# A decoder block on one core: first adaLN columns in three parts, four weight units side by side at both norms, per-token sums for the first norm

## The reference, cut to what matters

```python
mod = silu(c) @ w_ada + b_ada                    # 6144 columns: shift1, scale1, gate1, shift2, scale2, gate2
h   = rms_norm(x, norm1_g) * (1 + scale1) + shift1
proj = h @ w_in                                  # 128 columns of it are a "unit": units 0 to 3 are q_lat (2), k_idx, w_idx
...                                              # sparse attention, gated linear recurrence, merge
x   = x + gate1 * (merged @ w_out)
h2  = rms_norm(x, norm2_g) * (1 + scale2) + shift2
x   = x + gate2 * (square(relu(h2 @ w_mlp1 + b_mlp1)) @ w_mlp2 + b_mlp2)
```

## Time and profile before

| | us |
|---|---|
| three executions | 963.65, 968.84, 968.44 |
| median | 968.44 |
| the profiled execution | 967.11 |
| its span (first to last instruction) | 965.4 |
| PE, DVE, ACT, POOL busy in it | 878.1, 464.7, 335.9, 233.0 |
| mean granted clock of TensorE | 0.950 of full speed |

### The profile page before, as it was taken

One profiled execution on the slowest core, in us unless ns is written; L12 is line 12 of the kernel. 1 busy time (PEld: TensorE's weight loads), 2 busy tenths in 40 slices (PEclk: granted clock), 3 DMA queues, 4 the chain that ended last, 5 costly groups with the idle time before them and its releaser, 6 DMA issues.

```text
span 965.4 us, 10903 instructions
## 1 busy us (share of the span) xinstructions
PE 878.1 (91%) x3855; PEld 688.1 (71%) x3855; DVE 464.7 (48%) x763; ACT 335.9 (35%) x495; POOL 233.0 (24%) x125
## 2 busy tenths in 40 slices
PE   3799899899877977988899996999999999999998
PEld 2577578687766764655568874688888888888886
DVE  4914789791887784444429764643211122221000
ACT  2634452453123313665512223434312124442211
POOL 3024233334000000000000000264444444444440
PEclk9699999999989977989889998999999999999999
DMA  9912323423111112222226653263233233333302
GB/s 358 254 54 72 82 66 87 107 54 101 25 38 27 44 27 82 66 83 71 66 66 202 199 187 108 68 195 108 89 93 103 87 97 99 89 107 97 99 22 87
DMA packets 144551, 95.69 MB, mean 99 GB/s; under 512 B 8199, under 2 KB 138629, under 8 KB 143493
## 3 DMA queue, kind: packets, MB, share of 16 engines
q1 hardware_dynamic: 143104, 95.18, 33.2%
q10 hardware_dynamic: 1412, 0.07, 0.1%
HBM read 93.13 MB, written 2.10 MB: 99 GB/s over the span
## 4 chain that ended last, share of the span: by engine, by line
PE 75%; DVE 18%; DMA 2%; ACT 2%; issue 2%; SPq 0%; DVEq 0%; ACTq 0%
PE bank L1100 19%; PE bank L1101 19%; PE bank L1102 19%; PE bank L1241 3%; PE bank L1242 3%; PE bank L1243 2%; DMA ada_raw<-in_w_ada 2%; PE bank L1318 2%; PE bank L1344 2%; DVE w_lo L753 2%; DVE hg_at L909 2%; DVE hg_rt L877 1%; DVE rt_k L805 1%; PE bank L1128 1%; DVE ada_acc L972 1%
## 5 line engine op out<-in xcount | busy, mean ns | idle before, releaser
L407 POOL TENSOR_TENSOR w_lo<-w_raw,w_hi 128x1024 fp32r<-128x1024 f32 x90 | 224.1, 2489 | 703.7 <-ACT w_hi L461 703.7
L1100 PE MATMUL bank<-h_hi,w_hi 128*128 128x512 f32 x544 | 219.3, 403 | 14.0 <-DVE h_lo L783 13.5
L1101 PE MATMUL bank<-h_lo,w_hi 128*128 128x512 f32 x544 | 213.6, 393 | 0.0
L1102 PE MATMUL bank<-h_hi,w_lo 128*128 128x512 f32 x544 | 213.3, 392 | 0.0
L461 ACT ACTIVATE w_hi<-w_raw 128x1024 fp32r<-128x1024 f32 x126 | 132.7, 1053 | 166.1 <-PE bank L1102 163.5
L1100 PEld LDWEIGHTS bank<-h_hi,w_hi 128*128 128x128 f32 x544 | 102.9, 189 | 45.7 <-issue 16.9
L1101 PEld LDWEIGHTS bank<-h_lo,w_hi 128*128 128x128 f32 x544 | 103.3, 190 | 21.9 <-issue 1.7
L1102 PEld LDWEIGHTS bank<-h_hi,w_lo 128*128 128x128 f32 x544 | 103.2, 190 | 21.7
L1100 PE MATMUL bank<-u_hi,w_hi 128*128 128x512 f32 x256 | 100.0, 391 | 0.0
L1102 PE MATMUL bank<-u_hi,w_lo 128*128 128x512 f32 x256 | 99.7, 389 | 0.0
L1101 PE MATMUL bank<-u_lo,w_hi 128*128 128x512 f32 x256 | 99.6, 389 | 0.0
(11 more groups left out here) (212 smaller groups left out, 1087.1 us busy)
## 6 DMA issues: line engine op xcount, KB each, us to landing
w_raw<-in_w_mlp SPq DMA_DIRECT2D x128, 256.0 KB, 3.0
w_raw<-in_w_in SPq DMA_DIRECT2D x88, 256.0 KB, 3.3
ada_even<-in_w_ada SPq DMA_DIRECT2D x20, 512.0 KB, 4.7
ada_raw<-in_w_ada SPq DMA_DIRECT2D x8, 1024.0 KB, 9.1
ada_odd<-in_w_ada SPq DMA_DIRECT2D x8, 512.0 KB, 4.5
w_raw<-in_w_out SPq DMA_DIRECT2D x16, 256.0 KB, 3.0
x_nat<-in_x SPq DMA_DIRECT2D x4, 512.0 KB, 6.3
w_raw<-in_w_proj_a SPq DMA_DIRECT2D x8, 256.0 KB, 2.8
```

The costliest lines, as they stand in the source:

```text
L407: nc.gpsimd.tensor_tensor(w_lo[:, s], w_raw[:, s], w_hi[:, s].bitcast(F32), ALU.subtract).then_inc(lo_ready, 1)
L1100: mm(bank[b][:], w_hi[:, slot, j], rhs_hi(i), start=f, stop=False)
L1101: mm(bank[b][:], w_hi[:, slot, j], rhs_lo(i), start=False, stop=False)
L1102: end = mm(bank[b][:], w_lo[:, slot, j], rhs_hi(i), start=False, stop=l)
```

## The change

At the first norm the shift1 and scale1 columns are loaded, summed, turned and used in three parts of the feature tiles: tiles 0 to 3, 4 and 5, 6 and 7. SP's order becomes x, part 0 (eight DMAs of 512 KB, rows of 2 KB), weight units 0 to 3, part 1 and part 2 (eight DMAs of 256 KB each, rows of 1 KB). The sum of squares is taken from x as it lies in natural order: ACT squares and sums each 128 tokens in one instruction (four of 128x1024), a root and a reciprocal over 128x4 follow, DVE puts the four columns on diagonals, and four matmuls with ones spread them over a bank, which `scaled` then reads. The squares of the transposed tiles and their sums on PE go. Units 0 to 3 lie in banks 0 to 3 and are worked tile by tile: `block(n, k, b)` is three matmuls. Unit 5 waits for fewer read-outs. The two Exps on the lower bound move on ACT from the first stage to the place after the q roots.

At the second norm the first four units of w_mlp1 lie in banks 0, 1, 4 and 5; all four take tiles 0 to 2 as they come, then each its tiles 3 to 7. `mod_columns(2)` moves from before the last unit of w_out to around the last sum of squares, and DVE's use of it to after the reciprocal.

```diff
+    PARTS = [(0, 4), (4, 6), (6, 8)]
-            for k in range(KC):
-                if k >= 4:
-                    sp.wait_ge(ada_used, k - 3)
-                sp.dma_start(ada_raw[:, k % 4], w_ada_v[0, k]).then_inc(ada_loaded[k % 4], 16)
+            def load_ada1(part):
+                c0, c1 = PARTS[part]
+                for k in range(KC):
+                    if part:
+                        sp.wait_ge(ada_used, 4 * (part - 1) + k // 2 + 1)
+                    sp.dma_start(ada_raw[part][:, k], w_ada_v[k, :, 0:2, c0 * P:c1 * P]
+                                 ).then_inc(ada_loaded[KC * part + k], 16)
+            load_ada1(0)
...
             load(3, 3, columns(w_in_v, 3, ds(C_WIDX, P)))
+            load_ada1(1)
+            load_ada1(2)
...
+            for b in range(TB):
+                act.wait_ge(x_loaded[b], 16)
+                nc.scalar.activation(x_sq[:, b], x_nat[:, b], ACT.Square, accum_out=XSS[:, b:b + 1]
+                                     ).then_inc(xss_ready, 1)
+            nc.scalar.activation(XRS, XSS, ACT.Sqrt, scale=1.0 / D, bias=EPSC).then_inc(rt_ready, 1)
...
+            split_hi(0)
+            split_hi(1)
+            for part, (k0, k1) in enumerate(PARTS):
+                act.wait_ge(mod_ready, part + 1)
+                for k in range(k0, k1):
+                    act.wait_ge(t_ready, k + 1)
+                    nc.scalar.activation(h_hi[:, k], tmp[:, k % 2], ACT.Identity,
+                                         bias=SHIFT1[:, k:k + 1]).then_inc(t_hi, 1)
+                    if k in (1, 2):
+                        split_hi(k + 1)
...
             for k in range(KC):
+                ada_sum(0, k)
+                if k == 4:
+                    dve.wait_ge(rt_ready, 1)
+                    dve.wait_ge(consts_ready, 1)
+                    step(v.reciprocal(XRS, XRS))
+                    for b in range(TB):
+                        end = v.tensor_scalar(xr_diag[:, b], ident[:], XRS[:, b:b + 1], None, ALU.mult)
+                    end.then_inc(diag_ready, 1)
...
+            split_lo(0)
+            split_lo(1)
...
+            mod_part(0)
+            dve.wait_ge(xT_ready, KC)
+            dve.wait_ge(xrs_spread, 1)
+            norm_split(xT, A1, bank[6][:], SHIFT1, h_hi, h_lo, 4)
+            split_lo(2)
+            split_lo(3)
+            for k in range(KC):
+                ada_sum(1, k)
+            for k in range(3):
+                ada_sum(2, k)
+            mod_part(1)
+            norm_split(xT, A1, bank[6][:], SHIFT1, h_hi, h_lo, 6, 4)
+            for k in range(3, KC):
+                ada_sum(2, k)
+            mod_part(2)
+            norm_split(xT, A1, bank[6][:], SHIFT1, h_hi, h_lo, KC, 6)
...
-                if g >= 2:
-                    pe.wait_ge(lin_evac, g - 1)
+                pe.wait_ge(lin_evac, g - 1 if g >= 6 else g - 3)
...
+            def block(n, k, b):
+                mm(bank[b][:], w_hi[:, n % WS, k], h_hi[:, k], start=k == 0, stop=False)
+                mm(bank[b][:], w_hi[:, n % WS, k], h_lo[:, k], start=False, stop=False)
+                end = mm(bank[b][:], w_lo[:, n % WS, k], h_hi[:, k], start=False, stop=k == KC - 1)
+                if k == KC - 1:
+                    end.then_inc(group_done, 1)
+            mod_part(0)
+            for ns_ in ((0, 1), (2, 3)):
+                pe.wait_ge(lo_ready, ns_[1] + 1)
+                for k in range(4):
+                    pe.wait_ge(t_lo, k + 1)
+                    for n in ns_:
+                        block(n, k, n)
+            mod_part(1)
+            for k in range(4, 6):
+                pe.wait_ge(t_lo, k + 1)
+                for n in range(WS):
+                    block(n, k, n)
+            mod_part(2)
+            for n in range(WS):
+                for k in range(6, KC):
+                    pe.wait_ge(t_lo, k + 1)
+                    block(n, k, n)
+            unit(4)
...
-                if m == KC - 2:
-                    mod_columns(2)
+            mod_columns(2, 0, 4)
             sum_square(11, False, True, ones, sq_o)
+            mod_columns(2, 4, 8)
+            for k in range(3):
+                pe.wait_ge(t_lo, T_U - KC + k + 1)
+                for n in range(4):
+                    block(U_1[0] + n, k, UP_BANK[n])
+            for n in range(4):
+                for k in range(3, KC):
+                    if n == 0:
+                        pe.wait_ge(t_lo, T_U - KC + k + 1)
+                    block(U_1[0] + n, k, UP_BANK[n])
```

More of the change, by code:

```diff
@@ L492, in root @@
                                      bias=EPSC).then_inc(rt_ready, 1)
[L494 to L505, removed]
+            act.wait_ge(vec_turned, 1)
+            nc.scalar.activation(col[:], bank[0][:, 0:P], ACT.Copy).then_inc(col_ready, 1)
+            split_hi(0)
[8 more added lines that the diff above has]
+                        split_hi(k + 1)
             take(0, latT[:, 0]); split_hi(4)
@@ L669, in _ @@
                 split_hi(U_O + m + WS)
-            root(11, 26, rt_o[:], D)
+            root(11, 18, rt_o[:], D)
             for k in range(KC):
@@ L754, in split_lo, with mod_part, pair @@
                                 ALU.subtract).then_inc(lo_ready, 1)
[L756 to L763 removed]
+            split_lo(0)
+            split_lo(1)
+            def mod_part(part):
+                k0, k1 = PARTS[part]
+                def pair(t):
+                    return t.rearrange("p (s k) -> p s k", s=2)[:, :, k0:k1]
+                dve.wait_ge(mod_turned, part + 1)
+                step(v.tensor_tensor(pair(mod[:, 0:2 * KC]), pair(bank[7][:, 0:2 * KC]),
+                                     pair(col[:, V_BADA:V_BADA + 2 * KC]), ALU.add))
+                v.scalar_tensor_tensor(out=A1[:, k0:k1], in0=SCALE1[:, k0:k1], scalar=1.0,
+                                       in1=col[:, V_G1 + k0:V_G1 + k1], op0=ALU.add,
+                                       op1=ALU.mult).then_inc(mod_ready, 1)
+                dve.wait_ge(mod_ready, part + 1)
             nt = [0]
@@ L1142, in _ @@
                 end.then_inc(x_turned, 1)
-                if k:
-                    sum_square(0, k == 1, False, ones)
-            sum_square(0, False, True, ones)
-            pe.wait_ge(ada_used, KC)
-            for j in range(2 * KC):
-                end = mm(bank[1][:, j:j + 1], ada_acc[:, j * P:(j + 1) * P], ones[:, 0:1], start=True,
-                         stop=True)
-            end.then_inc(mod_turned, 1)
-            pe.wait_ge(mod_ready, 1)
-            unit(0, before=lambda k: pe.wait_ge(t_lo, k + 1))
@@ L1153, in _, with mod_part @@
-            for n in (1, 2, 3, 4):
-                unit(n)
+                if k == 3:
+                    pe.wait_ge(diag_ready, 1)
+                    for b in range(TB):
+                        end = mm(bank[6][:, b * P:(b + 1) * P], ones[:], xr_diag[:, b], start=True, stop=True)
+                    end.then_inc(xrs_spread, 1)
+            pe.wait_ge(vec_loaded, 16 * 15)
+            nc.tensor.transpose(bank[0][:, 0:P], vec[:], ident[:]).then_inc(vec_turned, 1)
+            def mod_part(part):
+                pe.wait_ge(ada_used, KC * (part + 1))
+                for j in range(*PARTS[part]):
+                    for g in range(2):
+                        end = mm(bank[7][:, g * KC + j:g * KC + j + 1], ada_acc[:, g, j * P:(j + 1) * P],
+                                 ones[:, 0:1], start=True, stop=True)
+                end.then_inc(mod_turned, 1)
```

159 lines of the change are left out of this document (80 added, 79 removed).

## The result

| | before | changed |
|---|---|---|
| executions beside each other | 963.65, 968.84, 968.44, 968.05, 963.35 | 962.09, 962.21, 962.05, 958.60, 958.03 |
| median | 968.05 | 962.05 |
| the profiled execution, its span | 967.11, 965.4 | 962.09, 960.3 |
| mean granted clock in it | 0.950 | 0.948 |

The ratio is 0.9924, with a 95% interval of 0.9904 to 0.9944: faster by about 7.4 us by the ratio and by 6.0 by the medians. 959.3 was forecast, with a range of 954 to 966. The direction and the range held; of the 9.1 us in the sum two thirds to four fifths came.

A forecast was written before the change was run, and what follows sets the result against it. PE, with 75% of the chain, was taken as the bound, time being gained where it waits or runs slowly. 4.1 + 1.1 + 3.9 = 9.1 off 967.11 gives 958.0, as a median 959.3, range 954 to 966.

The forecast's parts named there:

- Start of the norm: First norm: DVE begins it at 27.1 instead of 40.76, with 13.7 gained at the start, 10 of it from bytes.
- lies behind DVE's sums: First stage: the root's spread by four matmuls on PE was taken as covered by DVE's column sums.
- Small sums: First norm, DVE: column sums of 512 elements for parts 1 and 2 at 0.68 each, bounds 0.60 and 0.80.
- Rival (b): First norm: DVE's small sums have a floor, at worst 1.2 each; gain only 0.8, 967.6; chance 0.09.
- Clock: First norm: PE's gaps before tiles 4 and 6 bring the low clock back, costing 4.2 (3.3 to 5.0) of 8.3.
- Rival (a): First norm: both gaps leave the clock high; gain 13.3, so 955.1; chance 0.12.
- Rival (d): First norm: bursts of 24 matmuls never bring the full clock back; 5.2 slower, 973.6; chance 0.05.
- The mark: First norm: unit 3 read out at about 70.1 in the kernel before, the point its gain was measured from.
- Unit 5: After the first norm: unit 5 no longer waits for a read-out behind a square on ACT, gaining 1.1.
- rival (c): First stage DMA: short rows flow at the weights' 296 GB/s, norm 3.5 to 4 late; gain 5.3, 963.1; chance 0.11.
- Second norm: Tile 0 reaches PE 1.3 earlier and four units share the tiles: unit 3 read out at 625.8 against 629.7, gaining 3.9.
- Between the norms everything hangs on PE's flow and moves along: Stages between the two norms: assumed to shift along with PE, with no gain or loss entered for them.

The follow-up runs named there:

- after_again: The changed kernel run once more, unchanged: 960.89, ratio 0.9926 to the kernel before.
- first_norm_only: The changed kernel with its second norm put back as before: 965.83, ratio 0.9977 to the kernel before.
- fill_tuned: Changed kernel plus unused matmuls (fillers) at both norms, sums of squares of k and q, and attention heads 0, 3, 5, 7: 943.33, ratio 0.9725.
- two_parts_tuned: fill_tuned with the first norm's columns in two parts of four tiles, 10 fillers ahead of the turn, 12 behind: 944.04, ratio 0.9760.

## Why the prediction was right, and where it was off

**Start of the norm** (27.1, was 29.09). The bytes were right: part 0 was out of the way as a bound. The step that was short is "ACT's last copies and `col` end near 23.2": from the diagonals it allowed 4.4 and the trace has 6.3 (19.16 to 25.45). PE's spread of the root takes 2.08 of it, which "lies behind DVE's sums" had as covered, and the sixteen transposes of tiles 4 to 7 take 3.43 (21.23 to 24.66), so the last copy begins at 24.68 and everything behind follows it. They take 0.21 each; in the kernel before four start within 0.44, 0.11 each:

```profile
25.42 0.60 PE L1140 MATMUL bank<-ident,x_nat 128*128 128x128 f32 x4
25.86 1.02 PE L1128 MATMUL bank<-sq,ones 128*128 128x512 f32 x2
```

Half the pace looks like the low clock, but the row of the granted clock does not show it: in the changed kernel it reads 1.00 there. The cause of the slow transposes stays open.

```profile
21.30:24.60 3.30, 3.30 (x17) 1.00 1.26 267
```

Besides, a sum of 1024 elements has a pitch of 1.38 (14.04 - 12.66), not 1.2: I had taken overlap off where a dependent instruction adds 0.09 of waiting. These sums ended before the copies, so this did not set the start.

**Small sums** (0.68, was 0.85). Eleven of them took 37.5 to 46.0, 8.5 for 7.4. The instruction is 0.76, inside my bounds of 0.60 to 0.80; the pitch lies outside, because the bounds were durations and the list moves at the pitch of a chain. Rival (b) at 1.2 did not come.

**Clock.** In this profile it fell in both gaps, as forecast, and the runs with fillers price the two at about 2.9 (1.4 to 3.9 between single profiles) for 4.2 taken, with bounds of 3.3 to 5.0. The low stretches ran from 49.0 to 52.4 and from 59.3 to 62.6. Rival (a) is answered with the same runs: with a clock that stays up, about 3 more would have come. Half of it did come in `after_again`, where the gap ahead of tile 4 left the clock high. Rival (d) did not come: the clock was back within 4 us of each restart here, within 6 in `first_norm_only`. Against the sheet, tile 4 reached PE 1.9 late and tile 6 3.6 late; since the restarts cost less, the last group ends at 66.65 instead of 66.0. That this is so near is two errors of opposite sign, a start 2 too early and a clock about 1.3 too dear.

**The mark.** The 70.1 is the end of unit 3's last matmul, and as that it is right. As "unit 3 is read out" it was a misreading: ACT reads that bank (`wiT`) at 76.98 before and at 74.02 in the changed kernel, behind a square, so the sign "read out at 64 to 67" did not come. The forecast rests on the difference of the ends, so nothing else hangs on it.

**First norm in all:** 3.1 for 4.1. **Unit 5:** 0.6 for 1.1. ACT's read-out no longer holds it: in the timeline of PE it starts right behind the sums of squares, 4.0 earlier than before, and its first matmul takes 0.3 longer. The term was too large because I let these end at 76.6. The row of unit 5 has an idle of only 0.50, so they ended at 77.2.

**DMA.** The rows of 1 KB were taken at 350 GB/s. The stretches of all engines in the changed kernel, for rows of 2 KB, 1 KB and then 512 B:

```profile
8.00:19.00 11.00, 3.67 (x16) 3.27 (x16) 6.91 (x11) 8.74 (x16) 3.40 (x13) 1.00 1.05 383
...
30.00:40.00 10.00, 8.41 (x29) 6.84 (x30) 9.18 (x13) 4.50 (x6) 0.00 (x0) 0.73 1.11 347
40.00:46.00 6.00, 5.31 (x28) 4.45 (x27) 5.37 (x8) 0.00 (x0) 0.00 (x0) 1.00 1.20 292
```

383, 347 and 292, with 418 for 8 KB: in this kernel a transfer slows gradually as its rows get shorter. In DVE's timeline above no sum of parts 1 and 2 waits for a DMA, so rival (c) did not come. The Trainium skill (DMA: Bandwidth & Descriptors, Specifications) puts line rate at 512 B or more; these four numbers do not agree.

**Second norm** (3.9, was 3.6). The terms came as reasoned: tile 0 1.4 earlier for 1.3, PE idle 7.24, low clock behind it hidden no longer, read-outs 3.4 apart. For the moved Exps and SP's new order the profile shows no wait; the root's spread is the 2.08 above.

**Between the norms.** The failed step of the prediction is its last sentence of the sum: "Between the norms everything hangs on PE's flow and moves along." The work hangs on PE, but PE's speed there is not fixed. The timeline of PE in the changed kernel, at the sums of squares of the index stage:

```profile
96.92 4.49 PE L1177 MATMUL bank<-sq,twins 128*128 128x512 f32 x6 [2.15 <-ACT sq L502]
```

with a low clock after 2.15 idle; in the kernel before four of them took 1.98 after the same 2.15, and so did `after_again`:

```profile
95.48 1.98 PE L1177 MATMUL bank<-sq,twins 128*128 128x512 f32 x4 [2.15 <-ACT sq L502]
```

With such places at the first norm, in the index stage and in attention, two profiles of one kernel differ by 5 in span: `after_again` is 1.3 ahead of the changed kernel at unit 4, 2.8 at the first scores and 5.5 at the end of attention. The forecast of 958.0 for *the* profiled execution thus had an uncertainty of some 5 from this alone, and the agreement of medians to 3 us is partly luck. In profiled spans: 3.1 + 0.6 at the first norm, minus 3.6 up to 490, plus 1.6 up to 584, plus 3.6 is 5.3, against 5.1 in the spans.

## What to carry to other kernels

Price a chained instruction by the distance between starts in a chain, not by its duration, and price what comes ahead of the one that you moved (here the spread of the root and the transposes) as carefully as the move itself. When TensorE must wait a few microseconds for another engine, matmuls into a free bank that start before the clock falls may be worth more than the reordering: here they gave 17.6 us beyond the changed kernel run beside them, 960.89 to 943.33, where the change gave 6 to 7.4. First see whether PE sets the pace in that stage; where DVE does, a high clock buys nothing.

## What the runs showed of the hardware that was not expected

- The same idle of 2.15 us was followed by a low clock in one execution and not in another of the same code (above), and in `after_again` an idle of 2.84 left the clock high and one of 2.83 did not, so gaps of that length are a source of scatter. The 20 executions of the kernel before scatter over 6.4 us and the 12 of `first_norm_only` over 3.5; in both the longer spans mostly have the lower mean clock, in the six of `after_again` they do not.
- In attention, over nine profiles, 41.0 us of low clock went with 127.3 to 127.4 and 27.3 us with 123.6 to 123.7: 13.7 less of low clock for 3.7 less of time.
- In the recurrence the low clock of some 24 us cost nothing: 123.30 with it, 123.40 without.
- One-column matmuls take 0.22 at the low clock and 0.12 at the high one (3.57 and 1.95 for 16), so a turn of columns at the low clock costs nearly double.
- Fillers that begin at the low clock delay the real work: 0.42 each against 0.25. Beginning while the clock is high was not always enough: in `two_parts_tuned` it fell behind sixteen one-column matmuls and some fillers, with no more than 0.19 of idle. The Trainium skill (TensorE: Matmul & The Clock Gate, Why this matters for your kernels) advises against idle between bursts of matmuls; the runs agree, 0.9725 for `fill_tuned` against 0.9924 without.
